# Hybrid encoder with S5 mixer and PEER experts: rotation angles folded on ScalarE, three of eight drives on VectorE, C products interleaved, next layer's angle work moved to late blocks

## The chip, the cores and the metric

One core of one Trainium2 chip runs the whole program. The metric is the device time of one execution in microseconds (us), and the figure to compare is the median of several runs. Engines are named as the profile names them: PE is TensorE (PEld its weight loads), DVE is VectorE, ACT is ScalarE, POOL is GpSimd, SP is the engine that issues most transfers. A q behind a name is the engine's sequencer.

## The reference

Two layers on a sequence of 256 tokens of width 1024, then a final norm. A layer has a mixer (8 attention heads beside a bidirectional S5 with 32 channel groups) and PEER, which sums for every token 128 of 16384 single-neuron experts.

```python
for l in range(DEPTH):
    h = _rmsnorm(x, norm_mix[l])
    proj = h @ w_in[l]                      # q | k | v | u
    attn = _dilated_attention_mixture(q, k, v, rel_bias)
    # S5, forward and backward in time, per channel group:
    #   lam_bar = exp(lam * step);  state_t = lam_bar * state_(t-1) + B u_t
    #   y = Re(C state) + D u
    y = gelu(_s5_bidirectional(u, ...))
    ab = y @ w_glu[l]
    ssm = ab[..., :512] * sigmoid(ab[..., 512:])
    x = x + concat(_rmsnorm(attn), _rmsnorm(ssm)) @ w_out[l]
    x = x + _peer(_rmsnorm(x, norm_ffn[l]), w_query[l], sub_keys[l], expert_u[l], expert_v[l])
return _rmsnorm(x, norm_final)
```

PEER is computed densely: all 128 blocks of 128 experts are multiplied up (h with expert_u), gated by a matrix that is zero outside the chosen experts, and multiplied down (with expert_v). Everything is held to float32 accuracy; a float32 product in the experts is made of a high and a low part (u_hl, v_hl, w_hl, h_hl), in the mixer of two passes of a float32 matmul.

## The kernel before

Every engine has a stream written out by hand, and counting semaphores order the streams; nothing is scheduled by a planner. A layer runs in these stages: norm and projections, the mixer (about 120 us), its output products, eight retrieval heads with the first 48 up blocks (block c is 128 experts), the gates, the down products of blocks 0 to 47, then blocks 48 to 127, in which each step does the down product of block c and the up product of a block eight or four ahead.

**The mixer.** The S5 state is complex and has 4 quarters (q) of 8 tiles (n) of 128 state rows. The recurrence with a complex lam_bar is made a real one by turning the drive back by the angle that has accrued by time t, scanning with the real magnitude, and turning the state forward again. Tiles go in 16 pairs (g = 4q + s). For a pair the work is:

- `block_turns(g)` on DVE (lines 1476 to 1500): sum of a coarse and a fine angle in turns into bank 0 of PSUM (`TURN_BANK`), rounding, and subtraction of the rounded part into `tab`. It waits for the turned outputs that still read this place of `tab`.
- `angles(g)` on ACT (L1045): absolute value, sine, and cosine as the sine of a quarter turn less the absolute value; `s_tab` counts them.
- `b_pair` on PE (L644): B u into banks 5 and 6.
- `turn_in(q, n)` on DVE (L1505): B u times cos into `state`, B u times sin into `turn2`; two operations of 128x512 from PSUM; `s_pp`.
- `drives(q, n)` on POOL (L1882): two operations of 128x256 that add and subtract `turn2`; `s_drive`.
- `scan(q, n)` on DVE (L1520): two scans of 256 steps, `s_state`.
- `turn_out(q, n)` on POOL (L1888): state times cos into `outc`, state times sin into `outs`; two of 128x512 with four buffers each.
- `c_pair(q, p)` on PE (L649): eight float32 matmuls (16 passes in the profile's count), with 128 rows and 32 columns of weights; tile n goes to partitions 32(n%4) of bank 7. It waits until both kinds of output of both tiles are there.

All POOL instructions have the line L1847 and all DVE tensor-tensor operations L1355, that of a helper. The loop over g (DVE L1566, PE L763, POOL L1899) does on DVE: the turn-in of pair g+1, the scans of g, the angle work of g+3, and at s=1 the sum of the last quarter's y (L1549) and two row maxima of the scores (L1530), at s=0 the attention output (L1540). On PE it does, in this order, transposes of probabilities, a part of the projections of the next quarter (L622, L627), `b_pair` of g+2, `c_pair` of g-1, the rest of the projections, then scores (L675, L679) or values (L705). The last quarter has no projections and does gated products (L745) instead. ACT's order (L1096 on) puts between the angles of a quarter: copies of u, q, k, v, the exponentials (L1081), gelu (L1094) and copies of the transposed probabilities (L1087). SP waits for all turned outputs of a layer and then loads w_out.

**Angle work of a layer.** `step_angles`, `fine_angles` and `coefficients` on DVE (L1363 to L1443) make, from the parameters, the angles of 32 tiles times 32 (a coarse and a fine table of 1024 values a row), rounded to turns, and the coefficients. For layer 0 they stand before everything else of DVE; for the next layer they stand in the steps of blocks 49 to 55: `fine_angles` in four parts at blocks 50 to 53. In the last layer they are done too, for nothing. In the steps of blocks 56 to 123 DVE has the loop (L1804)

```python
weights(c, j % 2)
low_v(c, j % 2, v_raw[j % 2])
low_u(c + WIDE_AHEAD, j % 2)
pre_wide(i * 4 + j + 2, j % 2, WIDE_BANK[(j + 2) % 4])
```

with 17 turns of four blocks; PE does the down product (L893) and the wide up product (L850, L854, L857) of a block.

Of the kernel before, what the change touches and what calls it, by code (L numbers as in the profile page):

```python
# [22 lines left out]
ALU = mybir.AluOpType  # L23
# [10 lines left out]
NQ = 4  # L34
# [38 lines left out]
WIDE_AHEAD = 4  # L73
FIRST_V = (N_BATCH - 7, N_BATCH - 4)
# [4 lines left out]
def encoder(nc, x, w_in, w_out, w_glu, w_query, keys, expert_u, expert_v, rel_bias, gains,  # L79
            norm_final, ssm_par, ssm_b, ssm_c, consts, bucket_rows, out):  # L80
    ctx = ExitStack()
    with ctx:
# [13 lines left out]
        tiny = sb("tiny", [P, 4])  # L96
        eps_c, half_pi_c, one_c = tiny[:, 0:1], tiny[:, 1:2], tiny[:, 2:3]
# [47 lines left out]
        angle_t = c_low_f[:, 0:NQ * NT * 32].rearrange("p (n j) -> p n j", j=32)  # L145
# [29 lines left out]
        outs = [outs_a[:, 0, :, :], outs_a[:, 1, :, :], outs_b[:, 0, :, :], outs_b[:, 1, :, :]]  # L175
        w_out_sb = arena[:, big:big + DC * D].rearrange("p (k n) -> p k n", k=DC)
        xn = arena[:, big + DC * D:big + DC * D + TT * D].rearrange("p (a n) -> p a n", a=TT)
        b_f = take(NT * 2 * P)
# [43 lines left out]
        gfin = arena[:, TT * D:TT * D + D]  # L222
# [18 lines left out]
        FIRST_PAIRS = 3  # L241

# [39 lines left out]
        s_turns = sem("s_turns")  # L282
        s_tab = sem("s_tab")
# [6 lines left out]
        s_outc = sem("s_outc")  # L290
        s_y = sem("s_y")
# [71 lines left out]
        def _(sp):  # L363
# [52 lines left out]
            def layer(l, more):  # L416
# [157 lines left out]
        def _(pe):  # L574
# [20 lines left out]
            with pe.Fori(0, DEPTH) as l:  # L595
# [52 lines left out]

                def c_pair(q, p):  # L649
# [7 lines left out]
                    pe.wait_ge(s_outs, SLOTS + it * NT + 2 * p + 2)  # L657
                    for j, (kind, part) in enumerate(((0, 0), (1, 1), (2, 0), (2, 1))):
                        for n in (2 * p, 2 * p + 1):
                            k, o = n % 4, n // 4 * S  # L660
                            src = (outc, outs, outs, outc)[j][n % 4]
                            m = pe.matmul(ps[32 * k:32 * k + 32, 7, o:o + S], c_of(q, kind, n),
                                          src[:, part, :], start=(j == 0), stop=(j == 3))
                            if j == 3:
                                m.then_inc(s_y, 1)
# [85 lines left out]
                def glu_ahead(s):  # L751

                    if s == 1:
                        pe.wait_ge(s_turns, (l + 1) * NQ * PAIRS)
# [237 lines left out]
        def _(act):  # L992
# [39 lines left out]
            with act.Fori(0, DEPTH) as l:  # L1032
# [12 lines left out]
                def angles(g):  # L1045

                    tiles = slice(g % PAIRS * 2, g % PAIRS * 2 + 2)
                    act.wait_ge(s_turns, l * NQ * PAIRS + g + 1)
                    act.activation(tab[:, 1, tiles, :], tab[:, 0, tiles, :], ACT.Abs)
                    act.drain()  # L1050
                    act.activation(tab[:, 0, tiles, :], tab[:, 0, tiles, :], ACT.Sin, scale=TWO_PI_BELOW)
                    act.activation(tab[:, 1, tiles, :], tab[:, 1, tiles, :], ACT.Sin, scale=-TWO_PI_BELOW,
                                   bias=half_pi_c).then_inc(s_tab, 1)
# [278 lines left out]
        def _(dve):  # L1332
# [3 lines left out]
            dve.memset(one_c, 1.0)  # L1336
            dve.memset(half_pi_c, HALF_PI).then_inc(s_memset, 1)
# [3 lines left out]
            for counter in (s_u_mm, s_v_mm, s_gelu, s_pp, s_drive):  # L1341
                dve.sem_inc(counter, 2)
# [4 lines left out]
            dve.sem_inc(s_y, 4)  # L1347
# [39 lines left out]

            def fine_angles(part):

                if part == 0:  # L1390
                    dve.drain()
# [3 lines left out]
                    dve.drain()  # L1395
                    tt(angle, wide(11), ab, ALU.mult)
                if part == 1:
                    dve.drain()
                    dve.tensor_scalar(angle_t, angle, ROUND, ROUND, ALU.add, ALU.subtract)
                    dve.drain()  # L1400
                    tt(angle, angle, angle_t, ALU.subtract)
                if part == 2:
                    dve.drain()
# [596 lines left out]
```

## Time and profile before

| | us |
|---|---|
| median of 3 runs (lowest, highest) | 2082.67 (2080.65, 2087.59) |
| the profiled execution | 2079.7 |
| its span, first to last instruction | 2077.9 |
| PE busy | 2009.6 (97%) |
| PE weight loads busy | 1667.8 (80%) |
| DVE busy | 1636.4 (79%) |
| ACT busy | 1013.7 (49%) |
| POOL busy | 695.8 (33%) |

The mean granted clock of PE was 0.996 of full. "Busy" counts the time in which at least one instruction of an engine was under way; ends of matmuls are modelled, and an instruction's time may overlap that of the next. In views in order of time a line is a run of like instructions: start, length of the run, engine, source line, operation, what it writes and reads, shape, count; in brackets stands the idle time of the engine before it and what ended it. Stretches are told in us from the start of the span; the first layer's mixer lies from 21 to 165, the second's from 1049 to 1193.

### The profile page before, as it was taken

How to read it: one execution, taken by the hardware profiler on the slowest of the kernel's cores; microseconds unless marked ns; L12 is line 12 of the kernel's file. 1: busy time of each engine (PE TensorE's matmuls, PEld its weight loads, DVE VectorE, ACT ScalarE, POOL GpSimd, SP SyncE). 2: the span in 40 equal slices, each digit the busy share in tenths (PEclk: the TensorE clock that was granted, in tenths of full speed). 3: DMA queues.
4: the chain of work that ended last, by engine and by line, in shares of the span. 5: the costliest groups of instructions: out<-in, count | busy, mean ns of one | idle time of the engine just before them, and what ended most of it. 6: DMA issues, size and time to landing. Idle time of an engine off the chain costs nothing.

```text
span 2077.9 us, 37215 instructions
## 1 busy us (share of the span) xinstructions
PE 2009.6 (97%) x11470; PEld 1667.8 (80%) x11470; DVE 1636.4 (79%) x3058; ACT 1013.7 (49%) x1728; POOL 695.8 (33%) x535
## 2 busy tenths in 40 slices
PE   7999999998999999999999999999899999999998
PEld 5764999987887888888867559999778788888887
DVE  6992899886779977777779739998867788777776
ACT  4443554695355444444444435547933544444443
POOL 6992667671000400000049917776700012000000
PEclk9999999999999999999999999999999999999999
DMA  5223554214567555555423145541055665555553
GB/s 197 94 72 144 196 165 158 100 39 152 192 217 278 183 188 189 189 189 188 148 93 102 57 176 190 178 158 63 32 197 191 206 217 182 192 192 183 192 191 132
DMA packets 91276, 332.52 MB, mean 160 GB/s; under 512 B 10499, under 2 KB 14723, under 8 KB 88620
## 3 DMA queue, kind: packets, MB, share of 16 engines
q1 hardware_dynamic: 91164, 331.32, 47.2%
q8 instruction: 48, 0.79, 0.2%
q14 instruction: 48, 0.39, 0.1%
q10 hardware_dynamic: 16, 0.02, 0.0%
HBM read 326.04 MB, written 3.16 MB: 158 GB/s over the span
## 4 chain that ended last, share of the span: by engine, by line
PE 55%; DVE 15%; POOL 10%; issue 10%; DVEq 8%; ACT 1%; DMA 0%; POOLq 0%; ACTq 0%; SPq 0%
PE ps L893 31%; PE ps L850 12%; PE ps L854 5%; DVE arena L1355 5%; POOL arena L1847 5%; POOL v_raw L1847 4%; PE ps L793 3%; POOL u_raw L1847 2%; DVEq L1688 2%; DVE arena L1655 2%; DVE arena L1648 2%; DVE arena L1649 1%; PE ps L627 1%; DVEq L1680 1%; DVEq L1770 1%
## 5 line engine op out<-in xcount | busy, mean ns | idle before, releaser
L893 PE MATMUL ps<-v_hl,w_hl 128*128 128x512 f32 x3072 | 729.3, 391 | 12.7 <-DVE v_hl L1355 8.5
L893 PEld LDWEIGHTS ps<-v_hl,w_hl 128*128 128x128 f32 x3072 | 573.8, 188 | 139.9 <-DVE v_hl L1355 15.4
L850 PE MATMUL ps<-h_hl,u_hl 128*128 128x512 f32 x1152 | 418.3, 397 | 0.0
L1847 POOL TENSOR_TENSOR arena<-arena 128x256 f32<-128x256 f32 (+1 forms) x225 | 214.0, 994 | 370.0 <-DVE arena L1355 367.2
L1355 DVE TENSOR_TENSOR v_hl<-v_raw,v_hl 128x1024 fp32r<-128x1024 f32 x208 | 258.6, 1243 | 49.5 <-ACT v_hl L1178 45.5
L854 PE MATMUL ps<-h_hl,u_hl 128*128 128x256 f32 x1008 | 282.6, 280 | 0.0
L1178 ACT ACTIVATE v_hl<-v_raw 128x1024 fp32r<-128x1024 f32 x208 | 219.0, 1053 | 111.8 <-PE ps L893 94.2
L1355 DVE TENSOR_TENSOR u_hl<-u_raw,u_hl 128x1024 fp32r<-128x1024 f32 x144 | 180.2, 1252 | 111.0 <-ACT u_hl L1147 111.0
L850 PEld LDWEIGHTS ps<-h_hl,u_hl 128*128 128x128 f32 x1152 | 216.4, 188 | 45.1
L1147 ACT ACTIVATE u_hl<-u_raw 128x1024 fp32r<-128x1024 f32 x144 | 152.3, 1058 | 132.6 <-PE ps L850 131.7
L1290 ACT ACTIVATE act_w<-act_w 128x256 f32<-128x256 f32 x144 | 60.3, 418 | 302.2 <-DVE act_w L1790 302.2
L854 PEld LDWEIGHTS ps<-h_hl,u_hl 128*128 128x128 f32 x1008 | 190.2, 189 | 5.6
L1847 POOL TENSOR_TENSOR v_hl<-v_raw,v_hl 128x1024 fp32r<-128x1024 f32 x50 | 126.9, 2539 | 111.2 <-ACT v_hl L1158 111.2
L840 PE MATMUL ps<-h_hl,u_hl 128*128 128x256 f32 x1248 | 158.5, 285 | 0.0
L840 PEld LDWEIGHTS ps<-h_hl,u_hl 128*128 128x128 f32 x1248 | 153.0, 192 | 1.4
L1847 POOL TENSOR_TENSOR u_hl<-u_raw,u_hl 128x1024 fp32r<-128x1024 f32 x52 | 129.7, 2497 | 71.6 <-ACT u_hl L1158 71.6
L840 PE MATMUL ps<-h_hl,v_hl 128*128 128x256 f32 x1200 | 152.5, 285 | 0.0
L1847 POOL TENSOR_TENSOR v_raw<-v_raw,side 128x512 f32<-128x512 f32 x128 | 130.5, 1042 | 58.8 <-DVE v_raw L1355 58.8
L840 PEld LDWEIGHTS ps<-h_hl,v_hl 128*128 128x128 f32 x1200 | 147.1, 192 | 1.3
L1847 POOL TENSOR_TENSOR fence<-fence 128x1 f32<-128x1 f32 x3 | 2.5, 841 | 415.2 <-DVE w_hl L1355 399.5
L1355 DVE TENSOR_TENSOR arena<-arena 128x32 f32<-128x32 f32 (+4 forms) x120 | 113.6, 971 | 6.4 <-ACT arena L1008 3.2
L1355 DVE TENSOR_TENSOR arena<-ps,arena 128x512 f32<-128x512 f32 x164 | 101.8, 682 | 14.5 <-ACT arena L1133 5.0
(182 smaller groups left out, 2978.0 us busy)
## 6 DMA issues: line engine op xcount, KB each, us to landing
v_raw<-in_expert_v SPq DMA_DIRECT2D x208, 512.0 KB, 3.3
u_raw<-in_expert_u SPq DMA_DIRECT2D x206, 512.0 KB, 3.4
v_raw<-in_expert_u SPq DMA_DIRECT2D x50, 512.0 KB, 3.4
u_raw<-in_expert_v SPq DMA_DIRECT2D x48, 512.0 KB, 3.3
arena<-in_w_in SPq DMA_DIRECT2D x16, 512.0 KB, 3.8
arena<-in_w_in SPq DMA_DIRECT2D x8, 1024.0 KB, 5.0
arena<-in_ssm_b SPq DMA_DIRECT2D x16, 512.0 KB, 4.2
arena<-in_w_out SPq DMA_DIRECT2D x4, 2048.0 KB, 9.5
```

What stands on the lines that cost most here:

```text
L793: m = pe.matmul(ps[:, 4 + 2 * a + half, :], mixT[:, k, a * P:(a + 1) * P], w_out_sb[:, k, half * 512:(half + 1) * 512], start=(k == 0), st ...
L840: m = pe.matmul(ps[:, bank, o:o + S], hl[:, wp, k, :], h_hl[:, hp_, k, :], start=(k == 0 and j == 0), stop=(k == DC - 1 and j == 2))
L850: return pe.matmul(both, hl[:, 0, k, :], h_hl[:, :, k, :], start=(k == 0), stop=(k == DC - 1))
L854: pe.matmul(ps[:, bank, 0:S], hl[:, 1, k, :], h_hl[:, 0, k, :], start=False, stop=False)
L893: m = pe.matmul(ps[:, 2 * a + half, :], w_hl[s][:, wp, a * P:(a + 1) * P], v_hl[s][:, vp, half * 512:(half + 1) * 512], start=(first and j ...
L1147: act.activation(u_hl[s][:, 0, :, :], u_raw[s][:, :, :], ACT.Copy).then_inc(s_u_hi, 1)
L1178: act.activation(v_hl[s][:, 0, :], raw, ACT.Copy).then_inc(s_v_hi, 1)
L1290: act.activation(act_w[:, s, :], act_w[:, s, :], ACT.Gelu).then_inc(s_gelu, 1)
L1355: return dve.tensor_tensor(o, a, b, op)
L1648: dve.match_replace(b, v[:, 0:8], a, LOWEST)
L1655: m = dve.max_index(i[:, 8:16], v[:, 8:16], b)
L1847: return pool.tensor_tensor(o, a, b, op)
```

## The change

- `block_turns` keeps only the sum into bank 0, after a wait until ACT has read that bank (`s_turn_read`). ACT reads it twice with Abs, once shifted by a quarter turn, then folds both halves at once with a third Abs (less half a turn) and takes one Sin of 1024 elements. Both factors come out with their sign changed, which cancels between turn-in and turn-out. The wait for the turned outputs moves from DVE to ACT.
- For tiles 1, 3 and 5 of each quarter the drive is made on DVE: the sine product goes back into the PSUM bank, and after a drain two operations of 128x256 add and subtract it; the scan of such a tile is preceded by a drain. POOL keeps five of eight.
- `c_pair` does the cos products of its pair (two kinds), each followed by one of the two kinds of sin products of the pair before; the last pair of a quarter does its own sin products at the end. The semaphore `s_yc` counts the cos products. `outs` has six buffers for four.
- `fine_angles` has eight parts, with a second rounding and subtraction at the end, and uses `turn2` as scratch. For the next layer the parts stand behind the steps of blocks 116 to 123, one each, and those eight steps are written out behind a loop of 15 turns.
- The gain of the final norm is loaded into another place, behind another semaphore, at the same place of SP's stream.

```diff
+        outs = [outs_a[:, 0, :, :], outs_a[:, 1, :, :], outs_b[:, 0, :, :], outs_b[:, 1, :, :], act_w[:, :, :],
+                apart[:, :, :].rearrange("p j n -> p (j n)").rearrange("p (r t) -> p r t", r=2)]
+        DVE_TILES = (1, 3, 5)
 # SP
-                    sp.wait_ge(s_coef, l + 2)
+                    sp.wait_ge(s_wt, l * PK + GFIN_READ)
                     sp.dma_start(gfin, norm_final.partition_broadcast(P)).then_inc(s_gfin, 16)
 # PE
+                def c_product(q, n, j, src):
+                    k, o = n % 4, n // 4 * S
+                    kind, part = ((0, 0), (2, 1), (1, 1), (2, 0))[j]
+                    return pe.matmul(ps[32 * k:32 * k + 32, 7, o:o + S], c_of(q, kind, n), src[:, part, :],
+                                     start=(j == 0), stop=(j == 3))
                     pe.wait_ge(s_outc, SLOTS + it * NT + 2 * p + 2)
-                    pe.wait_ge(s_outs, SLOTS + it * NT + 2 * p + 2)
-                    for j, (kind, part) in enumerate(((0, 0), (1, 1), (2, 0), (2, 1))):
-...
+                    if p:
+                        pe.wait_ge(s_outs, SLOTS + it * NT + 2 * p)
+                    for j in range(2):
+                        for n in (2 * p, 2 * p + 1):
+                            m = c_product(q, n, j, outc[n % 4])
+                            if j:
+                                m.then_inc(s_yc, 1)
+                        if p:
+                            for n in (2 * p - 2, 2 * p - 1):
+                                m = c_product(q, n, 2 + j, outs[(q * NT + n) % SLOTS])
+                                if j:
+                                    m.then_inc(s_y, 1)
+                    if p == PAIRS - 1:
+                        pe.wait_ge(s_outs, SLOTS + it * NT + NT)
+...
 # ACT, angles(g)
+                    if g >= PAIRS:
+                        done = SLOTS + l * NQ * NT + 2 * (g - PAIRS + 1)
+                        act.wait_ge(s_outc, done)
+                        act.wait_ge(s_outs, done)
+                    act.activation(both[:, 1, :], ps[:, TURN_BANK, :], ACT.Abs)
+                    act.activation(both[:, 0, :], ps[:, TURN_BANK, :], ACT.Abs, bias=quarter_c).then_inc(s_turn_read, 1)
                     act.drain()
-...
+                    act.activation(both, both, ACT.Abs, bias=half_c)
+                    act.drain()
+                    act.activation(both, both, ACT.Sin, scale=-TWO_PI_BELOW, bias=half_pi_c).then_inc(s_tab, 1)
 # DVE, fine_angles(part)
+                if part == 1:
                     tt(angle, wide(11), ab, ALU.mult)
+                if part in (2, 6):
+                    dve.tensor_scalar(part_turns, angle, ROUND, ROUND, ALU.add, ALU.subtract)
+                if part in (3, 7):
+                    tt(angle, angle, part_turns, ALU.subtract)
+                if part == 4:
+                    tt(part_turns, wide(12), ab, ALU.mult)
+                if part == 5:
+                    tt(angle, angle, part_turns, ALU.add)
 # DVE, block_turns(g)
-                    dve.tensor_scalar(tab[:, 1, tiles, :], turns_ps, ROUND, ROUND, ALU.add, ALU.subtract)
-                    dve.drain()
-                    tt(tab[:, 0, tiles, :], turns_ps, tab[:, 1, tiles, :], ALU.subtract).then_inc(s_turns, 1)
+                    if g:
+                        dve.wait_ge(s_turn_read, l * NQ * PAIRS + g)
+                    tt(ps[:, TURN_BANK, :].rearrange("p (n a b) -> p n a b", n=2, a=16), a_part, b_part, ALU.add)\
+                        .then_inc(s_turns, 1)
 # DVE, turn_in(q, n)
+                    tt(z, bu, two(1, n), ALU.mult)
+                    if n in DVE_TILES:
+                        tt(bu, bu, two(0, n), ALU.mult)
+                        dve.drain()
+                        tt(z[:, 0, :], z[:, 0, :], bu[:, 1, :], ALU.add)
+                        tt(z[:, 1, :], z[:, 1, :], bu[:, 0, :], ALU.subtract).then_inc(s_pp, 1)
 # DVE, scan(q, n)
+                    if n in DVE_TILES:
+                        dve.drain()
 # DVE, late blocks
-                    if j in (2, 3, 4, 5):
-                        fine_angles(j - 2)
+                with dve.Fori(0, ANGLES_AT) as i:
+                    for j in range(4):
+                        late_block(i, j)
+                for j in range(8):
+                    late_block(ANGLES_AT + j // 4, j % 4)
+                    fine_angles(j)
 # POOL, turn_out(q, n)
+                    pool.wait_ge(s_yc, it * NT + n + 1)
+                    tt(outc[n % 4], state[:, (q * NT + n) % SLOTS, :, :], over(tab[:, 1, n, :], 2), ALU.mult)\
+                        .then_inc(s_outc, 1)
                     pool.wait_ge(s_y, it * NT + n + 1)
+                    tt(outs[(q * NT + n) % SLOTS], state[:, (q * NT + n) % SLOTS, :, :], over(tab[:, 0, n, :], 2),
+                       ALU.mult).then_inc(s_outs, 1)
```

## Rows read from the trace of the kernel before

**Rows 1.** The page: engines (part 1) and the chain of waits (part 4).

```profile
PE 2009.6 (97%) x11470; PEld 1667.8 (80%) x11470; DVE 1636.4 (79%) x3058; ACT 1013.7 (49%) x1728; POOL 695.8 (33%) x535
...
PE 55%; DVE 15%; POOL 10%; issue 10%; DVEq 8%; ACT 1%; DMA 0%; POOLq 0%; ACTq 0%; SPq 0%
```

**Rows 2.** Windows, mixer quarters; length, busy us of PE, PEld, DVE, ACT, POOL.

```profile
84.00:116.00 32.00, 32.00 (x213) 22.75 (x213) 30.34 (x54) 16.53 (x33) 30.87 (x33) 1.00 0.25 83
...
1116.00:1148.00 32.00, 32.00 (x214) 22.75 (x213) 30.26 (x54) 16.61 (x35) 30.86 (x33) 1.00 0.25 84
```

**Rows 3.** Order of time, PE, mixer quarter 1; start us, length us.

```profile
82.72 1.13 PE L679 MATMUL ps<-arena 64*128 64x256 f32 x8
...
86.34 1.92 PE L662 MATMUL ps<-arena 128*32 128x256 f32 x16
88.19 2.43 PE L627 MATMUL ps<-arena 128*128 128x256 f32 x10
...
109.27 3.72 PE L627 MATMUL ps<-arena 128*128 128x256 f32 x16
...
114.64 1.14 PE L679 MATMUL ps<-arena 64*128 64x256 f32 x8
```

**Rows 4.** Order of time, DVE, the same quarter.

```profile
82.11 0.42 DVE L1355 TENSOR_TENSOR arena<-arena,ps 128x256 f32<-128x256 f32 x1
...
83.89 0.69 DVE L1530 TENSOR_REDUCE arena<-ps 128x2 f32<-128x512 f32 x1 [0.18 <-PE ps L679]
...
93.55 0.69 DVE L1355 TENSOR_TENSOR ps<-arena,ps 128x512 f32<-128x512 f32 x1
...
95.22 3.08 DVE L1355 TENSOR_TENSOR arena<-ps,arena 128x512 f32<-128x512 f32 x5
```

**Rows 5.** Order of time, POOL, two pairs and the layer's last turns.

```profile
90.00 10.46 POOL L1847 TENSOR_TENSOR arena<-arena 128x256 f32<-128x256 f32 x12 [1.11 <-DVE arena L1355]
...
160.37 4.96 POOL L1847 TENSOR_TENSOR u_raw<-arena 128x512 f32<-128x512 f32 x4
```

**Rows 6.** Order of time, ACT, at the start and in quarter 1.

```profile
12.94 1.04 ACT L1030 ACTIVATE arena<-arena 128x1024 f32<-128x1024 f32 x1
...
89.17 0.62 ACT L1049 ACTIVATE arena<-arena 128x512 f32<-128x512 f32 x1
89.84 1.28 ACT L1051 ACT_TABLE_LOAD   x1
...
91.67 0.71 ACT L1052 ACTIVATE arena<-arena,tiny 128x512 f32<-128x512 f32 x1
92.28 0.58 ACT L1087 ACTIVATE arena<-ps 128x512 f32<-128x512 f32 x1
```

**Rows 7.** Order of time, DVE, first row maximum of the layer.

```profile
51.97 0.69 DVE L1530 TENSOR_REDUCE arena<-ps 128x2 f32<-128x512 f32 x1 [4.17 <-PE ps L679]
```

**Rows 8.** Order of time, PE, scores of quarter 3 and the last C group.

```profile
143.09 1.14 PE L679 MATMUL ps<-arena 64*128 64x256 f32 x8
...
165.47 1.92 PE L662 MATMUL ps<-u_raw,side 128*32 128x256 f32 x16 [1.94 <-POOL u_raw L1847]
```

**Rows 9.** Waits from 605 to 700 us, and a DVE step there.

```profile
PE ps L893 <- DVE v_hl L1355: 2.9, 3, 1.2
...
629.29 0.69 DVE L1399 TENSOR_SCALAR arena<-arena 128x1024 f32<-128x1024 f32 x1
```

**Rows 10.** Order of time, DVE, blocks 122 to 124, and PE at block 124.

```profile
1016.93 1.23 DVE L1355 TENSOR_TENSOR u_hl<-u_raw,u_hl 128x1024 fp32r<-128x1024 f32 x1 [1.07 <-ACT u_hl L1147]
...
1020.20 1.23 DVE L1355 TENSOR_TENSOR v_hl<-v_raw,v_hl 128x1024 fp32r<-128x1024 f32 x1 [0.24 <-ACT v_hl L1178]
...
1025.75 1.23 DVE L1355 TENSOR_TENSOR v_hl<-v_raw,v_hl 128x1024 fp32r<-128x1024 f32 x1 [0.27 <-ACT v_hl L1178]
...
1032.30 2.00 PE L893 MATMUL ps<-v_hl,w_hl 128*128 128x512 f32 x8
```

**Rows 11.** Order of time, DVE, first norm of the first layer.

```profile
15.99 0.17 DVE L1456 RECIPROCAL arena<-arena 128x1 f32<-128x1 f32 x1
```

More of the change, by code:

```diff
@@ L241, in encoder, with pool_drives @@
         FIRST_PAIRS = 3
+        DVE_TILES = (1, 3, 5)
+        POOL_TILES = NQ * (NT - len(DVE_TILES))
+        def pool_drives(m):
+            return sum(n % NT not in DVE_TILES for n in range(m))
         ps = ctx.enter_context(nc.psum_tensor("ps", [P, 8, 512], F32))
@@ L656, in c_pair @@
                     pe.wait_ge(s_outc, SLOTS + it * NT + 2 * p + 2)
-                    pe.wait_ge(s_outs, SLOTS + it * NT + 2 * p + 2)
-                    for j, (kind, part) in enumerate(((0, 0), (1, 1), (2, 0), (2, 1))):
+                    if p:
+                        pe.wait_ge(s_outs, SLOTS + it * NT + 2 * p)
+                    for j in range(2):
                         for n in (2 * p, 2 * p + 1):
[L660 to L665, printed above, removed]
+                            m = c_product(q, n, j, outc[n % 4])
[8 more added lines that the diff above has]
+                        pe.wait_ge(s_outs, SLOTS + it * NT + NT)
+                        for j in range(2):
+                            for n in (2 * p, 2 * p + 1):
+                                m = c_product(q, n, 2 + j, outs[(q * NT + n) % SLOTS])
+                                if j:
+                                    m.then_inc(s_y, 1)
                 def scores(q):
@@ L1340, in _ @@
             dve.sem_inc(s_gates, 4)
-            for counter in (s_u_mm, s_v_mm, s_gelu, s_pp, s_drive):
+            for counter in (s_u_mm, s_v_mm, s_gelu, s_pp):
                 dve.sem_inc(counter, 2)
@@ L1446, in _ @@
             step_angles(0)
-            for part in range(4):
+            for part in range(8):
                 fine_angles(part)
@@ L1478, in block_turns @@
                     q, p = divmod(g, PAIRS)
-                    tiles = slice(2 * p, 2 * p + 2)
                     some = angle[:, q * NT + 2 * p:q * NT + 2 * p + 2, :]
@@ L1890, in turn_out @@
                     pool.wait_ge(s_state, 2 * (it * NT + n + 1))
+                    pool.wait_ge(s_yc, it * NT + n + 1)
+                    tt(outc[n % 4], state[:, (q * NT + n) % SLOTS, :, :], over(tab[:, 1, n, :], 2), ALU.mult)\
+                        .then_inc(s_outc, 1)
                     pool.wait_ge(s_y, it * NT + n + 1)
-                    for dst, j, done in ((outc, 1, s_outc), (outs, 0, s_outs)):
-                        tt(dst[n % 4], state[:, (q * NT + n) % SLOTS, :, :], over(tab[:, j, n, :], 2), ALU.mult)\
-                            .then_inc(done, 1)
-                drives(0, 0)
-                drives(0, 1)
+                    tt(outs[(q * NT + n) % SLOTS], state[:, (q * NT + n) % SLOTS, :, :], over(tab[:, 0, n, :], 2),
+                       ALU.mult).then_inc(s_outs, 1)
+                for n in range(2):
+                    if n not in DVE_TILES:
+                        drives(0, n)
+                pool.wait_ge(s_toep_d, 16)
                 for g in range(NQ * PAIRS):
@@ L1901, in _ @@
                     if g + 1 < NQ * PAIRS:
-                        for j in range(2):
-                            drives((g + 1) // PAIRS, (g + 1) % PAIRS * 2 + j)
+                        for n in range((g + 1) % PAIRS * 2, (g + 1) % PAIRS * 2 + 2):
+                            if n not in DVE_TILES:
+                                drives((g + 1) // PAIRS, n)
                     for j in range(2):
```

80 lines of the change are left out of this document (34 added, 46 removed).

## The prediction

> **What bounds the kernel now.** The page comes first: PE is busy for 97% of the span, and the chain of waits gives 55% to PE, 15% to DVE and 10% to POOL [rows 1]. Such a share is an average, so the mixer, the stage that the change rewrites, has to be read by itself. A window of one of its quarters (32 us) shows PE, DVE and POOL busy for 32.0, 30.3 and 30.9 us, and the second layer repeats it [rows 2]. The chain calls these stretches POOL's, because POOL's work has no hole and the chain stays on an engine as long as nothing released it. PE's own order of time says more: from the scores of quarter 1 (82.72) to those of quarter 2 (114.64), 31.92 us, no group has idle time before it [rows 3]. VectorE is just as full: its row maximum starts at 83.89, waits 0.18 us for exactly those scores, and recurs after the same 32 us [rows 4]. So three engines run at one pace; PE sets it, DVE is 0.2 us and POOL about 1 us a quarter faster [rows 4, 5]. A saving on DVE and POOL alone buys nothing until the projections end.
>
> **Mixer, PE.** A 256-column pass costs a slot of 0.215 us: 16 take 3.72 us and 10 take 2.43, so six cost 1.29 [rows 3]. A C group is 16 passes in 1.92 us, that is eight slots with two passes each and a tail of 0.2: passes for different 32-column strips of the array already run two at a time [rows 3]. The new order puts the cos products of a pair between the sin products of the pair before, whose tiles own the other two strips. In a quarter the first group becomes 8 passes in 4 slots, the two middle ones 16 passes of four strips in 4 slots, the last one 4 slots and then 4 more for the late sin products: 20 slots for 32, 2.6 us less. No row shows four strips at once. Bounds: two at a time, 0 us; four, 2.6 us; a slot of fill per mixed group makes it 1.9. I take 2.6, since the second strip cost nothing over the first. The Trainium skill (TensorE: Matmul & The Clock Gate, Part 3: Packing small matmuls) reports 2.38 times for three column strips, not 3; by that a mixed group would need about five slots and the saving would be 1.9 us. The same section charges about 26 ns for each semaphore increment at the end of a pack; the two more per mixed group would be 0.3 us a layer, and no run here shows it.
>
> **Mixer, DVE.** Of a pair's angle work (93.55 to the end of the first of five operations, 95.82, 2.27 us) only the sum stays, 0.6 us and a semaphore: 1.6 us less, 6.4 a quarter. Three drives come in: two 128x256 operations each, estimated at 0.33 us a step (a 128x512 operation lasts 0.69 and steps by 0.60, the 128x256 one lasts 0.42), plus two drains at 0.16: 1.0 us, 3.0 a quarter. 31.9 becomes 28.5 us [rows 4]. **POOL** loses six 128x256 operations of 0.69 us a quarter, 4.1 of 30.6 us: twelve operations, eight of this form and four of 128x512, take 10.46 [rows 5]. Both drop below PE.
>
> **Mixer, ACT.** Each pair now takes two Abs from PSUM (0.58), one Abs and one Sin of 1,024 elements (1.04 for the nearest row, 1.15 assumed for Sin) in place of an Abs (0.62) and two Sins (0.71) of 512: 3.6 us for about 2.0 [rows 6]. ACT has room (16.5 us busy in a quarter [rows 2]), but one place is a loop. After the row maximum (R) come the exponentials and gelu; the next Abs starts at R+5.3 now (83.89 to 89.17). After the change it is Abs, Abs, Abs (to R+7.8), table load (1.28), Sin: the table of the fourth pair on is ready at R+10.3 [rows 6]. DVE wants it at R+9.1 (0.6+1.3+0.8+0.7 to the end of its iteration, then 5.7 for the next). It stalls 1.2 us, and from there to the next R are 28.5-9.1=19.4 us: the loop is 29.7 us. PE needs 31.9-2.6=29.3, plus 0.4 for B products that wait for the late turn. I take 29.8 us a quarter.
>
> **Sum of a mixer.** Up to 52 us PE sets the pace (DVE waits 4.17 us for the first scores [rows 7]) and nothing is gained. Quarter 1's R falls to 83.9-2.6=81.3, quarter 2's to 111.1, quarter 3's to 140.9 (PE's scores would be there at 136.5: 143.09+1.1 less 7.7 [rows 8]). After that R POOL has 4.9 (two turns out), 2.7 (two drives) and 9.8 (four turns out): 17.5 us. The last turn ends at 158.4 where it now ends at 165.3 (160.37+4.96 [rows 5]): 6.9 us a layer, 13.8 in all. The last C group (165.47, 1.92 us [rows 8]) has only its four late products behind POOL: 0.9 us a layer, 1.8. Its cover is none: PE is the path from there.
>
> **Angle work moved.** At blocks 50 to 53 DVE loses four parts (four operations of 1,024 elements at 1.23 us, one at 0.69, and some 0.7 us of small ones and drains: 6.3 us [rows 9, 10]). PE waits three times there for the low half of V, 2.9 us, in each layer [rows 9]. I book all of it, 5.7 us; at least 3.3, if the third wait (1.2 us, behind the coefficients, which stay) is not cured. In blocks 116 to 123 DVE gains one part a block: five at 1.3 us, two at 0.77, one at 0.5. DVE idles 1.07+0.24 us in a block there, and it is far ahead: the low half for block 124 is ready at 1026.98, PE takes it at 1032.30 [rows 10]. Cost 0; if neither slack held, 8.0 us a layer. Before the first layer two more operations of 1,024 elements stand on DVE's way to the first norm, and DVE reaches that norm at 15.99 with no idle time before it [rows 11]: 0.77+1.3 (the steps above), so 2.1 us, once. The copied semaphores, the two memsets, the new place of the final gain (still loaded behind the last V block on SP, nothing is queued behind it), POOL's wait for a scratch that has long been written, and one extra wait of DVE for ACT's read of the bank a pair earlier are covered by the engines' slack: 0.
>
> **The numbers.** -13.8-1.8-5.7+2.1 = -19.2 us. The profiled execution took 2079.7 us around its span of 2077.9 and gives 2060.5; the median of the runs is 3.0 us above it, 2082.7, and gives 2063.5.
>
> **Rivals.**
> Two strips at a time (20%): C groups cost PE what they cost now. PE holds quarter 2's R at 115.8; the last quarter has no projections and runs at 29.8: 145.6, end 163.1, 2.2 us a layer. -4.4-1.8-5.7+2.1 = -9.8: 2072.9. For it: no row has more than two at once. Against: strips share nothing the rows can see.
> The chain is right and POOL sets the pace (7%): 4.1 us in each of eight quarters, -33-1.8-5.7+2.1 = -38: 2044. Against: PE's order of time without a hole.
> The late blocks are full (8%): 8.0 us a layer beside the forecast, -3: 2079.5. For it: 1.30 us of work against 1.31 of idle time. Against: 5.3 us of lead.
> Slower: four strips get into each other's way and the mixed groups run in single file (5%). A quarter then has 4+16+16+20=56 slots for 32, 5.2 us more on PE; R of quarter 3 goes to 144.2+15.5=159.7, the end to 177.2, +11.9 a layer, in all +18: 2101. It decides from about 2.1 us more a quarter, a mean C group of 2.45 us for 1.92. Against: two strips don't disturb each other.
>
> **How the numbers follow.** The forecast has 60%: 2058 to 2070 by its own terms (fill slots, a Sin longer than assumed, 3.3 instead of 5.7). With the two-strip case and part of the others 8 in 10 lie in 2052 to 2080. About 0.3%, 6.2 us, is what a measurement of this kernel tells from no change. Faster by more: the forecast, the POOL case and most of the two-strip case, 0.83; within it 0.10; slower 0.07.
>
> **What would show it.** Scores of quarters 1 and 2 about 29.8 us apart; mixed C groups of 16 passes in 1.1 to 1.3 us (1.9 is the second case, above 3 the slower one); a DVE wait of about 1.2 us for ACT's Sin once a quarter; last turn out near 158.4 plus the 2.1 of the start; no PE waits for V in blocks 48 to 56 and none in 116 to 127. It is wrong if the quarter stays at 31.9, if DVE waits for the tables of other pairs too (ACT as the bound), or if PE waits for v_hl near the end of a layer.

## The result, and the profile after

The changed kernel takes 2071.2 us (median of 6 runs, 2069.2 to 2074.5) beside 2087.5 us for the kernel before on the same chip: ratio 0.9934, 95% interval 0.9916 to 0.9952, or 13.7 us less (10 to 17.5) of 2085. The ratio is that of the means, and one run of the kernel before, at 8475.55 us where its others took 2080.7 to 2087.7, is left out of it. Run again with the last experiments the changed kernel gives 0.9935 [0.9918, 0.9952]. The forecast was 19.2 us less, 2063.5 us with 2058 to 2070 by its own terms. 13.7 us off the forecast's own base of 2082.7 make 2069.0, inside that range; the median itself is 1.2 us above that range. The profiled execution took 2070.0 us around a span of 2068.2, 9.7 us less than the one of before.

The page, parts 1 and 4, and windows of the changed kernel (columns as in [rows 2], then the granted clock of TensorE, DMA share and GB/s):

```profile
PE 1998.5 (97%) x11470; PEld 1663.8 (80%) x11470; DVE 1618.5 (78%) x3050; ACT 1062.3 (51%) x1760; POOL 662.9 (32%) x487
...
PE 62%; DVE 13%; issue 9%; DVEq 7%; POOL 6%; ACT 2%; DMA 1%; ACTq 0%; POOLq 0%; SPq 0%
```

```profile
84.00:116.00 32.00, 30.95 (x223) 22.49 (x223) 28.87 (x55) 23.58 (x41) 27.65 (x28) 1.00 0.24 84
116.00:148.00 32.00, 29.93 (x216) 19.71 (x212) 29.37 (x56) 23.16 (x39) 28.58 (x29) 1.00 0.24 83
...
155.50:165.70 10.20, 9.09 (x50) 4.54 (x51) 2.90 (x10) 4.28 (x8) 6.13 (x5) 0.50 0.31 103
...
1176.00:1186.30 10.30, 8.62 (x50) 4.42 (x51) 2.54 (x10) 4.20 (x7) 6.69 (x6) 0.50 0.24 80
```

In a mixer quarter no engine is quite full any more (before, three were or nearly so, [rows 2]). The last two lines show 10.2 us at the end of each mixer at a granted clock of 0.50, TensorE's level of 1.2 GHz. The kernel before had 3.4 us of it there, from 146.8 and from 1174.2, and ran its last two C groups at full clock:

```profile
146.80:150.20 3.40, 3.40 (x18) 1.28 (x16) 3.40 (x7) 1.10 (x5) 3.38 (x4) 0.50 0.02 5
```

VectorE in order of time: the first norm, then row maxima and one wait:

```profile
18.27 0.17 DVE L1490 RECIPROCAL arena<-arena 128x1 f32<-128x1 f32 x1
...
83.52 0.69 DVE L1568 TENSOR_REDUCE arena<-ps 128x2 f32<-128x512 f32 x1 [0.73 <-PE ps L705]
...
94.13 1.89 DVE L1390 TENSOR_TENSOR arena<-ps,arena 128x512 f32<-128x512 f32 x3 [1.34 <-ACT arena L1085]
...
113.98 0.69 DVE L1568 TENSOR_REDUCE arena<-ps 128x2 f32<-128x512 f32 x1
...
143.96 0.67 DVE L1568 TENSOR_REDUCE arena<-ps 128x2 f32<-128x512 f32 x1
```

The first norm is 2.28 us later than in [rows 11]. The row maximum of quarter 0 is at 54.16 here, so those of quarters 1 to 3 follow it by 29.36, 59.82 and 89.80 us; before, they followed by 31.92, 63.83 and 95.69. Once a quarter VectorE waits 1.34 us for ScalarE's Sin.

TensorE and POOL at the end of the mixer (L662 are C products, L771 the attention half of the gated projection, L819 the output projection):

```profile
148.15 0.41 PE L662 MATMUL ps<-u_raw,side 128*32 128x256 f32 x2
148.16 0.41 PE L662 MATMUL ps<-arena,side 128*32 128x256 f32 x2
...
148.83 0.39 PE L662 MATMUL ps<-arena,side 128*32 128x256 f32 x2
...
155.54 0.64 PE L662 MATMUL ps<-arena,side 128*32 128x256 f32 x2 [2.73 <-POOL arena L1890]
...
160.44 0.64 PE L662 MATMUL ps<-u_raw,side 128*32 128x256 f32 x2 [1.06 <-POOL u_raw L1890]
...
162.15 1.92 PE L662 MATMUL ps<-arena,side 128*32 128x256 f32 x8
164.00 6.25 PE L771 MATMUL ps<-arena 128*128 128x512 f32 x12
...
174.39 1.88 PE L819 MATMUL ps<-arena 128*128 128x512 f32 x4
```

```profile
144.12 4.96 POOL L1890 TENSOR_TENSOR u_raw<-arena 128x512 f32<-128x512 f32 x4 [2.19 <-DVE arena L1563]
...
160.34 1.29 POOL L1890 TENSOR_TENSOR arena<-arena 128x512 f32<-128x512 f32 x1
```

Four strips share the array: the mixed group from 148.15 has 16 passes and ends 1.07 us later, little more than half of the 1.92 in [rows 3]. After a wait of 2.73 us the next groups run at half the clock: eight late passes take 1.92 us, the projection 6.25. The kernel before waited 1.08 us for its third group and ran the same projection in 5.42:

```profile
160.57 1.92 PE L662 MATMUL ps<-arena,side 128*32 128x256 f32 x16 [1.08 <-POOL arena L1847]
...
167.32 5.42 PE L745 MATMUL ps<-arena 128*128 128x512 f32 x12
```

The waits from 605 to 700 us (total, times, longest), the first line in the kernel before and the others in the changed one, and TensorE at late block 124 of the changed kernel:

```profile
PEld ps L893 <- DVE v_hl L1355: 5.7, 8, 1.6
```

```profile
ACT v_hl L1210 <- DMA v_raw<-in_expert_v: 7.5, 5, 2.0
...
PE ps L919 <- DVE v_hl L1390: 1.3, 1, 1.3
```

```profile
1028.27 5.97 PE L919 MATMUL ps<-v_hl,w_hl 128*128 128x512 f32 x25
```

Of the three waits of [rows 9] one is left in layer 0, and behind it stands a transfer of V; in layer 1 none is left. The late blocks run with no wait for V: block 124 of layer 0 is 4.03 us ahead of [rows 10], as is block 56, so the eight angle parts cost nothing.

Where the 9.7 us of the two profiles lie (times of the same matmul after less before, us):

| stretch | layer 0 | layer 1 | foreseen a layer |
|---|---|---|---|
| start of the program, to the first scores | +2.2 | | +2.1 |
| first scores to output projection | -4.7 | -4.9 | -7.8 |
| output projection to block 48 (nothing changed there) | +0.5 | +3.2 | 0 |
| blocks 48 to 56 | -2.1 | -4.1 | -2.85 |

The measured entries add up to -9.9; the 0.2 us that are left lie behind block 56.

### The profile page after: what moved, and what is told of

Read it like the earlier page. It is cut to its first block, busy times and chain, and to the rows that moved or that the text cites. A ratio compares the mean times of both kernels' runs of the same rounds, so it can differ in the third digit from the quotient of the medians.

```text
span 2068.2 us, 37197 instructions
## 1 busy us (share of the span) xinstructions
PE 1998.5 (97%) x11470; PEld 1663.8 (80%) x11470; DVE 1618.5 (78%) x3050; ACT 1062.3 (51%) x1760; POOL 662.9 (32%) x487
## 4 chain that ended last, share of the span: by engine, by line
PE 62%; DVE 13%; issue 9%; DVEq 7%; POOL 6%; ACT 2%; DMA 1%; ACTq 0%; POOLq 0%; SPq 0%
PE ps L919 32%; PE ps L876 12%; PE ps L880 5%; DVE arena L1390 4%; POOL v_raw L1890 4%; PE ps L819 3%; PE ps L636 2%; DVEq L1726 2%; DVE arena L1693 2%; DVE arena L1686 2%; PE ps L631 1%; DVE arena L1687 1%; POOL arena L1890 1%; PE ps L662 1%; PE ps L653 1%
## 5 line engine op out<-in xcount | busy, mean ns | idle before, releaser
L1890 POOL TENSOR_TENSOR arena<-arena 128x512 f32<-128x512 f32 (+1 forms) x169 | 171.6, 1041 | 370.4 <-DVE arena L1390 362.3
L1390 DVE TENSOR_TENSOR arena<-arena 128x32 f32<-128x32 f32 (+3 forms) x123 | 117.3, 978 | 6.9 <-ACT arena L1034 3.4
L1390 DVE TENSOR_TENSOR arena<-arena,ps 128x192 f32<-128x192 f32 (+2 forms) x200 | 75.9, 396 | 43.4 <-PE ps L985 24.8
```

The source lines that it names most:

```text
L1390: return dve.tensor_tensor(o, a, b, op)
L1890: return pool.tensor_tensor(o, a, b, op)
```

## The experiments

All ratios are to the kernel before on the same chip. "R" is the distance from the first row maximum of a layer to that of quarters 1, 2, 3; for one kernel it repeats between layers, and for the changed kernel between runs on two chips, within 0.04 us (for `pairs_only` within 0.5). "POOL" is the distance to the end of the last turn out, "out" that from the end of the first scores to the output projection (layer 0, layer 1).

| kernel | ratio [95%] | R | POOL | out |
|---|---|---|---|---|
| before | 1 | 31.92, 63.83, 95.69 | 113.4 | 124.9, 125.0 |
| changed | 0.9934 [0.9916, 0.9952] | 29.35, 59.82, 89.80 | 107.5 | 120.3, 120.0 |
| pairs_only | 1.0003 [0.9992, 1.0013] | 32.33, 64.13, 95.98 | 113.6 | 126.4, 125.5 |
| move_only | 0.9976 [0.9964, 0.9987] | 31.91, 63.86, 95.84 | 113.5 | 126.7, 125.1 |
| after_single | 0.9968 [0.9956, 0.9981] | 31.91, 63.83, 93.80 | 111.5 | 124.7, 123.1 |
| folded_only | 0.9977 [0.9967, 0.9987] | 31.91, 63.83, 92.75 | 111.6 | 123.2, 123.2 |
| no_dve_tiles | 0.9937 [0.9924, 0.9951] | 29.35, 58.70, 86.84 | 109.2 | 121.0, 121.4 |
| keep | 0.9920 [0.9905, 0.9934] | 29.35, 59.81, 89.79 | 107.5 | 119.4, 119.7 |
| last_out | 0.9913 [0.9898, 0.9928] | 29.35, 59.81, 89.79 | 103.4 | 118.1, 119.5 |
| late_bias | 0.9924 [0.9911, 0.9938] | 29.35, 59.82, 89.81 | 107.5 | 119.4, 120.4 |
| best | 0.9889 [0.9874, 0.9904] | 29.35, 59.82, 89.80 | 103.5 | 116.2, 116.2 |
| best2 | 0.9894 [0.9879, 0.9910] | 29.35, 59.81, 89.78 | 105.2 | 116.2, 116.2 |

**pairs_only**: the kernel before with the new order of C products alone (and the six sin buffers that it needs).

```diff
+                    for j in range(2):
+                        for n in (2 * p, 2 * p + 1):
+                            m = c_product(q, n, j, outc[n % 4])
...
+                            for n in (2 * p - 2, 2 * p - 1):
+                                m = c_product(q, n, 2 + j, outs[(q * NT + n) % SLOTS])
```

> The kernel before with the paired C products alone (six sin buffers, a separate count for the freed cos buffers). Theory (TensorE, VectorE and POOL all need 31 to 32 us a quarter, so relief of one alone is worth nothing): the mixed C groups take 1.07 us for 16 passes, yet the scores of the quarters stay 31.5 to 32 us apart; only the last C group of a layer gains, about 1 us, so 1 to 3 us under the kernel before in all. Rival (TensorE alone sets the pace and the others follow it): quarters of 29.3 us, 2.6 us in each of three quarters a layer, 16 to 18 us under the kernel before.

Measured: no difference (-2 to +3 us), and row maxima 31.8 us apart (84.04 and 115.84 in this trace):

```profile
84.04 0.69 DVE L1550 TENSOR_REDUCE arena<-ps 128x2 f32<-128x512 f32 x1 [0.44 <-PE ps L698]
...
115.84 0.66 DVE L1550 TENSOR_REDUCE arena<-ps 128x2 f32<-128x512 f32 x1
```

In quarter 2, which ran at full clock, VectorE does not wait for the scores: it is the pace with its 31.8 us. Quarter 1 took 32.33 us in layer 0, with 3.4 us at a granted clock of 0.50 in it (from 66.9). Even the small gain foreseen did not come: from 159.1, in layer 0, TensorE ran at 0.50 for 10.2 us, as in the changed kernel. The mean granted clock of its runs was 0.990, that of the kernel before 0.994, so the ratio alone would not show that the pairing is worth nothing; the row maxima do.

**after_single** and **folded_only** take the pairing out of the changed kernel; the second also sets `DVE_TILES = ()`.

```diff
+                    pe.wait_ge(s_outs, SLOTS + it * NT + 2 * p + 2)
+                    for j in range(4):
+                        for n in (2 * p, 2 * p + 1):
+                            src = outc[n % 4] if j < 2 else outs[(q * NT + n) % SLOTS]
+                            m = c_product(q, n, j, src)
```

> The changed kernel with the C products of a pair issued together again (four passes for each of the two tiles, no mixing with the pair before), all else kept. Theory (without the pairing TensorE is the bound again at 31.9 us a quarter while VectorE and POOL are free): scores 31.9 us apart, the last turn out leaves POOL 2 to 4 us later than in the changed kernel, 4 to 9 us over the changed kernel in all. Rival (the loop of ScalarE and VectorE sets the pace in the changed kernel, and pairing is idle there): within 2 us of the changed kernel, quarters of 30 us.

> The changed kernel with the C products of a pair issued together again and all eight drives on POOL: of the edits to the mixer only the folded angles and the six sin buffers stay. Theory (TensorE holds the quarter at 31.9 us, POOL needs 30.7, VectorE is free): scores 31.9 us apart, the row maximum of the last quarter 93.8 us behind that of the first as with the single C products, the last turn out 19 to 20 us behind it as POOL has a backlog; 1 us or so gained a mixer, 3 to 5 us under the kernel before in all, most of it from the up blocks. Rival (the folded angles are what made the mixer faster): as fast as the changed kernel within 2 us.

Measured: 7 us over the changed kernel (0.9968 against 0.9934), and 9 us with all drives on POOL; the intervals of the two meet. TensorE is the pace again at 31.91 us, and VectorE waits for it:

```profile
117.89 0.69 DVE L1556 TENSOR_REDUCE arena<-ps 128x2 f32<-128x512 f32 x1 [1.50 <-PE ps L693]
```

So TensorE's relief is worth nothing alone, VectorE's and POOL's 1.9 us of POOL's path a layer, and all together 5.9. In folded_only, where POOL is not relieved at all, the path is 1.8 us shorter, so the 1.9 are VectorE's. They come in the last quarter, where TensorE has no projections: the first two distances stay 31.91 and 63.83, the third falls to 92.75 (93.8 was foreseen).

**no_dve_tiles**: the changed kernel with `DVE_TILES = ()`.

> The changed kernel with all eight drives of a quarter on POOL again, the folded angles and the paired C products kept. Theory (POOL then needs 30.6 to 30.9 us a quarter as before, VectorE about 26): POOL sets the pace, its busy time has no hole, scores 30.7 us apart, the row maximum of the last quarter 1.5 to 2.5 us later, 3 to 5 us over the changed kernel in all. Rival (TensorE and the loop of ScalarE and VectorE hold the quarter at 29.5 to 30.5 us anyway): within 1.5 us of the changed kernel.

Measured: 0.9937, no difference from the changed kernel that this can tell. The theory fails but for POOL's work without a hole. Row maxima come as fast as TensorE allows, earlier than in the changed kernel:

```profile
83.81 0.69 DVE L1568 TENSOR_REDUCE arena<-ps 128x2 f32<-128x512 f32 x1 [2.91 <-PE ps L705]
...
113.16 0.69 DVE L1568 TENSOR_REDUCE arena<-ps 128x2 f32<-128x512 f32 x1 [2.18 <-PE ps L705]
...
141.30 0.67 DVE L1568 TENSOR_REDUCE arena<-ps 128x2 f32<-128x512 f32 x1
```

POOL drags a backlog behind them and ends 22.4 us after the last one, not 17.7: at 109.2, 1.8 us later than with three drives on VectorE. So it is the drives on VectorE that make its loop with ScalarE the pace (30.46 and 29.98 us for quarters 2 and 3, without them 29.35 and 28.14), and moving them shortens POOL's path by 1.8 us a layer, not by their 4.1 us a quarter.

**keep**: the changed kernel with matmuls of constants in TensorE's waits of the last quarter.

```diff
+                    if q == NQ - 1 and p == PAIRS - 2:
+                        pe.wait_ge(s_pp, 2 + (l + 1) * NQ * NT)
+                        keep_busy(5, 5)
+                    if q == NQ - 1 and p == PAIRS - 1:
+                        keep_busy(2, 5)
```

> The changed kernel with seven extra matmuls of constants on TensorE in the last quarter of each mixer, five where it waits 2.7 us before the third C group and two where it waits 1.1 us before the last; they write a bank that nobody reads. Theory (in the changed kernel TensorE idles more in the last quarter, the granted clock falls to 0.5 for 10.2 us of every mixer where it was 3.4 us before, and the last C group, the attention projection and the output projection run at 1.2 GHz): no such stretch, the last C group in about 1.9 us instead of 3.6, the output projection begins 2 to 2.5 us earlier, 4 to 5 us under the changed kernel in all. Rival (the clock falls there whatever TensorE does, or the stretch hides behind POOL's turns out): within 1 us of the changed kernel, the stretch still there. Rival (the extra matmuls come in the way): 1 to 2 us slower.

Measured: 3 us under the changed kernel where 4 to 5 were foreseen (0.9920 against 0.9934 and 0.9935; the intervals overlap), mean granted clock of its runs 0.995 against 0.990. A window of the same stretch:

```profile
155.50:165.70 10.20, 8.31 (x50) 4.06 (x43) 2.99 (x10) 5.85 (x10) 5.41 (x5) 0.83 0.38 135
```

One stretch of 3.4 us at 0.50 is left, from 160.2, behind a wait of 1.89 us before the last group, so the output projection comes only 0.9 and 0.3 us earlier. That is 1.2 of the 2.9 us; this profile is the slowest of the six runs (2072.6 us, the others 2065.3 to 2070.1), and where the others gained the rest is not shown. Nor do 0.9 us in one layer prove much: late_bias, which fills no wait, has the same 119.4 us in layer 0, because the clock held past its wait of 2.74 us there and fell for only 3.4 us, from 162.1:

```profile
156.61 0.41 PE L670 MATMUL ps<-arena,side 128*32 128x256 f32 x2 [2.74 <-POOL arena L1898]
```

What tells is the count over all traces. The five traces with the new tail and nothing in its waits (changed, after_again, no_dve_tiles, last_out, late_bias) have ten mixer ends, with half clock for 10.2 us in seven, 6.8 in two and 3.4 in one; the three with the waits filled (keep, best, best2) have six, with 3.4 us in two and none in four.

**last_out**: the last two tiles of a layer are turned out by VectorE.

```diff
+                for n in range(NT - 2, NT):
...
+                    tt(outc[n % 4], z, over(tab[:, 1, n, :], 2), ALU.mult)
...
+                    tt(outs[m % SLOTS], z, over(tab[:, 0, n, :], 2), ALU.mult)
...
+                for counter in (s_outc, s_outs):
+                    dve.wait_ge(counter, SLOTS + it * NT + NT - 2)
+                    dve.sem_inc(counter, 2)
```

> The changed kernel with the turns out of the last two of the 32 tiles of a layer on VectorE, which is idle there, in place of POOL. Theory (in the last quarter POOL's 16 operations after the last row maximum, 17.5 us without a hole, are the path to the end of the mixer): POOL ends 4.9 us earlier, VectorE does the same four operations in 2.5 us behind its last scan and ends at about the same time, the last C group ends 4 to 5 us earlier a layer, 8 to 10 us under the changed kernel in all. Rival (VectorE is late itself, or the copy of the probabilities and TensorE's low clock are the path): 2 us a layer or less, 0 to 4 in all.

Measured: 4.4 us under the changed kernel, half of the theory, with intervals that overlap; in the profile the output projection comes 2.2 and 0.5 us earlier. VectorE and POOL in order of time:

```profile
153.32 0.89 DVE L1390 TENSOR_TENSOR u_raw<-arena 128x512 f32<-128x512 f32 x1
154.13 1.75 DVE L1390 TENSOR_TENSOR arena<-arena 128x512 f32<-128x512 f32 x1
155.80 1.76 DVE L1390 TENSOR_TENSOR u_raw<-arena 128x512 f32<-128x512 f32 x1
157.48 0.68 DVE L1390 TENSOR_TENSOR arena<-arena 128x512 f32<-128x512 f32 x1
```

```profile
152.41 1.25 POOL L1903 TENSOR_TENSOR act_w<-arena 128x512 f32<-128x512 f32 x1
153.63 1.70 POOL L1903 TENSOR_TENSOR arena<-arena 128x512 f32<-128x512 f32 x1
155.29 1.72 POOL L1903 TENSOR_TENSOR apart<-arena 128x512 f32<-128x512 f32 x1
```

VectorE's product lasts 1.75 us while POOL runs and 0.68 once POOL is done; POOL's grows from 1.25 to 1.72. Side by side each engine starts a product every 1.67 us, so the two do little more than they would in turn (0.68 and 1.25, 1.93 us for both). VectorE ends at 158.16, some 2 us later than four products of 0.6 us from 153.32 and a POOL at its old pace would allow (155.8 and 156.1, an estimate from these rows). The clock still falls, for 6.8 and 10.2 us.

**move_only** and **late_bias** are about the up blocks: the first is the kernel before with only the new `fine_angles` in blocks 116 to 123 (and the new place of the final gain), the second the changed kernel with this:

```diff
-                    sp.dma_start(bias, overlap).then_inc(s_bias, 16)
...
+                for i in range(4):
+                    late_loads(i + 1)
+                    if more:
+                        load_bias(i)
```

> The kernel before with the angle work of the next layer moved alone (eight parts in the late up blocks). Theory (read from the two traces: 4.1 us a layer come back at blocks 50 to 53, because the wait for the low half of V is longer than the idle time of TensorE shows; the late blocks cost nothing; the start costs 2.3 us once): 2.3-8.2=-5.9 us against the kernel before, or -3.8 if one V transfer is late again in one layer. Rival (the figure of the prediction, the idle time alone): 2.1-5.7=-3.6 us. Rival (the late blocks are full): +4 us or more, with TensorE waiting for the low half of V from block 116 on.

> The changed kernel with the load of the next layer's bias windows (1.5 MB) cut into four and issued one after each pair of late up blocks behind block 58, not whole at block 54. Theory (in layer 0 the idle time that the angle work left at blocks 50 to 53 is taken by a V transfer that lands behind this load, the DMA engines being 95 to 100% busy; layer 1 has no such load and keeps its whole gain of 4.1 us): the V wait at block 54 goes, 2 to 4 us under the changed kernel. Rival (the V transfer is late for the 3 MB of projections and residual loaded ahead of it): within 1 us of the changed kernel, the wait still there. Rival (the four parts collide with the late V blocks): as long a wait, later.

Measured: move_only takes 5.0 us off (2.7 to 7.5), which cannot tell the theory's 5.9 us from its 3.8 or from the rival's 3.6; the trace can. Blocks 48 to 56, 34.7 us before, take 30.8 in layer 1 (3.9 less) and 35.0 in layer 0, where nothing is gained. ScalarE, TensorE and a window there:

```profile
647.40 1.06 ACT L1179 ACTIVATE v_hl<-v_raw 128x1024 fp32r<-128x1024 f32 x1 [3.20 <-DMA v_raw<-in_expert_v]
...
649.77 2.50 PE L894 MATMUL ps<-v_hl,w_hl 128*128 128x512 f32 x5 [2.28 <-DVE v_hl L1356]
```

```profile
636.00:648.00 12.00, 11.49 (x55) 9.27 (x54) 9.42 (x26) 4.63 (x7) 0.00 (x0) 1.00 0.96 340
```

With late_bias the same window shows the DMA engines at 0.64, and TensorE takes the 24 matmuls of two blocks in 5.73 us without a hole. The eight blocks of layer 0 last 32.6 to 35.3 us in the eight traces with the angles moved and the load whole, and 31.0 to 31.5 in the three with it cut. Of the eight, the five at 34.6 to 35.3 us (move_only's is one) have 3.4 us at a granted clock of 0.50 behind that wait; the three without, the changed kernel's two among them, take 32.6 to 33.4. So the late transfer costs 1 to 2 us by itself, and some 2 more where the clock falls behind it.

```profile
636.00:648.00 12.00, 12.00 (x59) 9.94 (x58) 10.81 (x32) 5.70 (x7) 0.00 (x0) 1.00 0.64 199
```

```profile
641.25 5.73 PE L927 MATMUL ps<-v_hl,w_hl 128*128 128x512 f32 x24
```

In time it is 2.1 us under the changed kernel, inside the intervals of both.

**after_again**, the changed kernel once more.

> The changed kernel itself, beside the others of this call. Theory (the profile of the changed kernel has three stretches of 3.4 us at a granted clock of 0.5 outside the mixers, and one of 10.2 us in each mixer): the stretches in the mixers are there again, 7 to 10 us long; in layer 0 the V transfer behind the bias load is late by 2 to 4 us again and in layer 1 not; ratio to the kernel before 0.993 to 0.9945. Rival (both are accidents of one execution): no such stretch, no late V.

Measured: 0.9935; 10.2 us at 0.50 from 155.3 and from 1179.3, and a wait of TensorE of 2.3 us for V in layer 0 alone. Three stretches of 3.4 us again, one at the same place (476) and two elsewhere (1056 and 1500, where the first trace had 1231 and 1504). The mean clock moves from run to run in the kernel before too: its 25 runs beside pairs_only average 2088.9, 2085.0, 2083.9 and 2081.6 us at mean granted clocks of 0.993 (3 runs), 0.994 (12), 0.995 (8) and 0.996 (2).

**best** joins last_out, late_bias and keep (five and one); **best2** also drives the last tile on VectorE and gives tile 30 back to POOL.

> The changed kernel with three of the edits together: the last two turns out on VectorE, the bias windows loaded late in four parts, and matmuls of constants in TensorE's waits of the last quarter (five before the third C group, one before the last). Theory (the three work on different stretches, and the clock stretch is shorter): 8 to 10 us for the first, 2 to 4 for the second, 1 to 3 for the third, so 12 to 16 us under the changed kernel, about 2056 us. Rival (the end of the mixer has another path as soon as POOL is shorter): 6 us or less under it.

> The fastest version so far, with the last tile of a layer driven on VectorE too and only that tile turned out there; POOL turns out tile 30 again. Theory (multiplications on VectorE with both operands in SBUF last 1.21 us there and POOL's 1.22 instead of 1.09 while both run, so POOL with 12 and VectorE with 4 of them end at 157.0 and 158.2; one tile less for VectorE ends both near 157): the last C group ends 1 us earlier a layer, 1.5 to 2.5 us under that version. Rival (POOL and VectorE slow each other by what they do together, whoever does it): no change, within 1 us.

Measured: best is 9.4 us under the changed kernel, less than the 12 to 16 foreseen as last_out gave half of its 8 to 10, and 23 under the kernel before, at 2062.1 us. The three measured alone, 4.4, 2.1 and 2.9, add up to it, to the tenth by luck: each is uncertain by some 3 us. At the end of neither mixer does its clock fall:

```profile
155.50:165.70 10.20, 9.87 (x66) 5.08 (x59) 5.42 (x13) 5.21 (x10) 1.37 (x1) 1.00 0.65 246
```

best2 is no faster: POOL's last two products, at 1.72 us, ran beside VectorE's, and POOL ended 1.7 us later. Its theory's figures for POOL, 1.22 us instead of 1.09, stand in no row: a product of POOL starts 1.23 us after the last alone and 1.67 beside VectorE's. The rival holds.

```profile
156.90 1.72 POOL L1920 TENSOR_TENSOR u_raw<-arena 128x512 f32<-128x512 f32 x1
158.58 1.72 POOL L1920 TENSOR_TENSOR arena<-arena 128x512 f32<-128x512 f32 x1
```

## Why the prediction was right, and where not

**The number.** 13.7 us is nearer to the 9.8 of the rival with two strips than to the 19.2 of the forecast. The time alone could not have told them apart; the C groups in the trace do.

**What bounds the mixer: right for TensorE and VectorE.** They run at one pace, and POOL, which the chain of waits names, does not set it. pairs_only (TensorE relieved) gives nothing, after_single (VectorE and POOL relieved) 1.9 us of path a layer, all together 5.9. POOL's relief counts only at the end of a layer: without it (no_dve_tiles) 4.1 of the 5.9 come.

**Four strips at once: right.** A mixed group took 1.07 us, where 1.1 to 1.3 were named, and the quarter that TensorE paces fell by 2.56 us (2.6). The figure of the Trainium skill that was weighed against it (TensorE: Matmul & The Clock Gate, Part 3: Packing small matmuls, three column strips 2.38 times as fast) would, by the prediction's estimate, have meant five slots; the trace shows four. The rival of two strips and the one in single file fall. Of the 0.3 us a layer for more semaphore increments nothing is seen: a mixed group, with four, took 1.07 us, and the first group of a quarter, with two, 1.06 (from 143.09). By its own rate that term was 0.6 us: a layer has 12 mixed groups.

**The loop of ScalarE and VectorE: right in kind, 0.4 us a quarter short.** The Sin wait was put at 1.2 and is 1.34 us; quarters 2 and 3 were put at 29.8 and are 30.46 and 29.98. The table came 10.6 us behind the row maximum (10.3 foreseen), and VectorE's way from there to the next was 19.8 and 19.4 us (19.4 foreseen). The last row maximum gained 5.9 us where 6.7 were foreseen, and the POOL work behind it lasted 17.7 us (17.5).

**The tail of a layer: the step that failed.** "Has only its four late products behind POOL: 0.9 us a layer" took TensorE's clock as given. With POOL's pace unchanged at the end and less to do before, TensorE waits 2.73 us for the third group, where it waited 1.08 in the kernel before (at 160.57), and the clock then is 0.50 for 10.2 us. That an unfilled wait brings the fall rests on the count of mixer ends (see keep): 3.4 to 10.2 us at half clock in all ten with the waits open, none or 3.4 in the six with them filled. It is not certain in each execution, and its length varies. The distance from POOL's end to that of the C products grew from 2.07 to 2.44 us, not fell to 1.2, and the projection took 6.25 and 6.01 us, not 5.42. With the 1.0 us by which POOL's path fell short of its 6.9, most of it the loop, that is the missing 3 us a layer. In best, at full clock, the last eight passes take 1.03 us and the projection 5.42.

**V waits: mis-sized, and one given back.** They were booked at TensorE's idle time, 2.85 us a layer. In layer 1 the kernels with the angles moved gain 3.3 to 4.1: the matmuls' own line of 2.9 us [rows 9] leaves out what their weight loads waited, 5.7 us by the line shown above, and the length of the blocks would have told the loss. In layer 0 something else was late next, which the prediction did not name: the V transfer queued behind the 1.5 MB bias load, with the DMA engines 96% busy in move_only's trace. One of its signs, no wait of TensorE for V in blocks 48 to 56, failed there. The two errors cancel by luck: 6.2 us in this profile, 5.7 foreseen.

**Start, late blocks: right.** +2.2 for +2.1; 0 for 0.

**Stretches at half clock elsewhere**: the output projection to block 48 took 3.7 us more in the two layers, which no step had. Three stretches of 3.4 us lie there (from 476.3, 1230.7 and 1503.7) and none in the profile of before; matched with those of before, the matmuls fall back by 1.0 to 1.6 us in each. The profile of before is one of its fastest executions (mean granted clock 0.996; its runs average 0.994), so the difference of the two profiles, 9.7 us, understates the 13.7 of the ratio.

Open: why the clock falls more often outside the mixers in some executions than in others, and what the three drives are worth: POOL's path says 1.8 us a layer, the times nothing.

## What to carry to other kernels

Where several engines run at one pace, take the relief of each alone as zero for as long as they do, and look for the loop that the next one closes. A stage whose pace-setter gets faster leaves TensorE waiting at its end; price the matmuls behind that wait at both clocks, and fill the wait if it can be filled. Before calling such a fall the work of one edit, count it over all traces of the tail, since it comes and goes between executions. When a wait goes, read the DMA queue of that stretch: a stall of 4 us can hide a transfer that is just as late.

## What the runs showed of the hardware

Products of 128x512 with both operands in SBUF lasted 0.68 us on VectorE with POOL idle and 1.75 with POOL busy, and POOL's went from 1.25 to 1.72. The Trainium skill (SBUF — State Buffer, Who interferes with whom) states that a VectorE instruction with two SBUF inputs contends with a GpSimd one that reads SBUF; the trace agrees, though both engines slow down here rather than one alone. VectorE's products that read one operand from PSUM kept their 0.69 us beside POOL [rows 4, 5], and so did the drives that moved to VectorE, each with an operand in PSUM: 0.69 and 0.42 us an operation in the changed kernel's trace, whether POOL was busy or not.
